# The opening phase of a two-layer transformer kernel: evictions shared by two engines, products with the identity ahead of the turns, one-column sums and a first weight chunk in halves

## The reference, cut to what matters

```python
c_act = jax.nn.silu(c)
mod = c_act @ w_ada + b_ada
shift_mix, scale_mix, gate_mix, ... = jnp.split(mod, N_MOD, axis=-1)
h = rms_norm(x) * (1 + scale_mix) + shift_mix
proj = h @ w_in
# second block, both of its layers (a and b):
kv = rmsnorm(mem, mem_norm) @ w_mem_kv
```

## Time and profile before

| what | value |
|---|---|
| median of 3 runs | 1800.53 us (1800.51 to 1802.06) |
| the profiled execution's own time | 1800.57 us |
| its span, first to last instruction | 1798.9 us |
| TensorE busy | 1768.7 us, 98% of the span |
| VectorE busy | 1096.3 us, 61% |
| ScalarE busy | 733.2 us, 41% |
| share of PE in the chain that ended last | 92% |

### The profile page before, as it was taken

How to read it: one execution, slowest core, us unless ns; L and a number is a source line. 1 busy time by engine, 2 the same in 40 slices (tenths; PEclk the granted TensorE clock), 3 DMA queues, 4 the chain that set the end, 5 groups by cost and what they waited for, 6 DMA issues and landing times.

```text
span 1798.9 us, 22457 instructions
## 1 busy us (share of the span) xinstructions
PE 1768.7 (98%) x8312; PEld 1428.7 (79%) x8312; DVE 1096.3 (61%) x1598; ACT 733.2 (41%) x1030; POOL 40.6 (2%) x78
## 2 busy tenths in 40 slices
PE   7999999999999999999999999999999999999998
PEld 6887547888888888878888888889766888888887
DVE  6878775655556335775677674245577567677423
ACT  7313663333444223444344443233365434444322
POOL 4110000000000000000000000000000000000000
PEclk9999999999999999999999999999999999999999
DMA  9794203232222323312322222323401232222231
GB/s 345 266 340 139 80 21 111 75 106 94 93 93 87 111 82 98 112 48 94 117 93 93 93 93 84 109 83 106 170 24 48 74 114 93 93 93 93 94 105 70
DMA packets 149081, 195.29 MB, mean 109 GB/s; under 512 B 3646, under 2 KB 133000, under 8 KB 146332
## 3 DMA queue, kind: packets, MB, share of 16 engines
q1 hardware_dynamic: 140696, 154.23, 26.4%
q0 software_dynamic: 7600, 39.13, 5.9%
q10 hardware_dynamic: 724, 1.10, 0.2%
HBM read 189.15 MB, written 5.29 MB: 108 GB/s over the span
## 4 chain that ended last, share of the span: by engine, by line
PE 92%; DVE 4%; DMA 2%; ACT 1%; issue 1%; POOL 0%; DVEq 0%; ACTq 0%
PE bank L805 20%; PE bank L807 20%; PE bank L806 20%; PE bank L868 3%; PE bank L870 3%; PE bank L869 3%; PE bank L1475 2%; PE bank L1474 2%; PE bank L1476 2%; PE bank L952 2%; PE bank L1004 1%; PE bank L848 1%; PE bank L973 1%; PE bank L849 1%; PE bank L850 1%; PE bank L1061 1%
## 5 line engine op out<-in xcount | busy, mean ns | idle before, releaser
L1947 DVE TENSOR_TENSOR w_lo<-w_stage,w_hi 128x2048 fp32r<-128x2048 f32 (+3 forms) x136 | 299.0, 2198 | 436.3 <-ACT w_hi L1502 436.0
L805 PE MATMUL bank<-act_hi,w_hi 128*128 128x512 f32 x1216 | 475.2, 391 | 1.5 <-DVE act_lo L2322 0.6
L807 PE MATMUL bank<-act_hi,w_lo 128*128 128x512 f32 x1216 | 473.3, 389 | 0.0
L806 PE MATMUL bank<-act_lo,w_hi 128*128 128x512 f32 x1216 | 473.1, 389 | 0.0
L1502 ACT ACTIVATE w_hi<-w_stage 128x2048 fp32r<-128x2048 f32 (+3 forms) x138 | 253.6, 1837 | 466.0 <-PE bank L807 335.6
L805 PEld LDWEIGHTS bank<-act_hi,w_hi 128*128 128x128 f32 x1216 | 228.2, 188 | 50.7 <-DVE act_lo L2011 2.1
L806 PEld LDWEIGHTS bank<-act_lo,w_hi 128*128 128x128 f32 x1216 | 228.3, 188 | 47.7 <-issue 0.5
L807 PEld LDWEIGHTS bank<-act_hi,w_lo 128*128 128x128 f32 x1216 | 228.2, 188 | 47.7
L805 PE MATMUL bank<-mid_hi,w_hi 128*128 128x512 f32 x352 | 136.9, 389 | 0.0
L806 PE MATMUL bank<-mid_lo,w_hi 128*128 128x512 f32 x352 | 136.9, 389 | 0.0
L807 PE MATMUL bank<-mid_hi,w_lo 128*128 128x512 f32 x352 | 136.9, 389 | 0.0
(11 more groups left out here) (412 smaller groups left out, 2622.8 us busy)
## 6 DMA issues: line engine op xcount, KB each, us to landing
ada_stage<-in_w_ada POOLq DMA_DIRECT2D x24, 1024.0 KB, 7.4
w_stage<-in_w_up SPq DMA_DIRECT2D x22, 1024.0 KB, 5.0
w_stage<-in_a_ffn_in SPq DMA_DIRECT2D x22, 1024.0 KB, 5.0
w_stage<-in_b_ffn_in SPq DMA_DIRECT2D x22, 1024.0 KB, 5.1
w_stage<-in_w_in SPq DMA_DIRECT2D x10, 1024.0 KB, 7.6
w_stage<-in_b_ffn_out SPq DMA_DIRECT2D x10, 1024.0 KB, 5.1
w_stage<-in_w_down SPq DMA_DIRECT2D x8, 1024.0 KB, 5.1
w_stage<-in_a_ffn_out SPq DMA_DIRECT2D x8, 1024.0 KB, 5.1
```

What stands on the lines that cost most here:

```text
L805: pe.matmul(dst, wh, mh, start=start and k == 0, stop=False)
L806: pe.matmul(dst, wh, ml, start=False, stop=False)
L807: last = pe.matmul(dst, wl, mh, start=False, stop=stop and k == nk - 1)
L1947: dve.tensor_tensor(w_lo[slot][:, 0:n], raw[:, 0:n], w_hi[slot][:, 0:n].bitcast(FP32), ALU.subtract).then_inc(w_ready, 1)
```

## The change

It touches only the opening phase.

1. Ahead of the turn of the gains, behind the wait for their rows, TensorE multiplies the identity by itself 16 times (`WARM`), and 8 times more ahead of the turns of `x` (`WARM_X`). Nothing reads the results.
2. The even tiles of the memory are evicted by ACT, the odd ones by DVE.
3. The squares of `x` are summed by ACT (two token tiles) and DVE (two), on both behind their evictions of the memory.
4. ACT computes silu of `c` behind the root of `x`, and one table load is gone.
5. SP issues `w_mem` when the first piece of `w_ada` has landed, instead of at the start.
6. The eight column blocks of `scale_mix` are summed by eight products with a column of ones, one output column each, instead of eight turns and a reduction on DVE.
7. The first chunk is split in halves of 1024 columns, and TensorE goes through it tile k by tile k for both output tiles.

```diff
+WARM, WARM_X = 16, 8
...
+            sp.wait_ge(ada_loaded[0], 16)
+            load_mem(0)
...
             pe.wait_ge(vec_loaded, 16 * (len(VECTORS) + 1))
+            for i in range(WARM):
+                pe.matmul(bank[0][:, 0:P], ident[:, :], ident[:, :], start=True, stop=True)
             sizes = [N_VEC, 48] + [2 * CT] * 6
             batch("vec", 0, [(vec_rows[0:sizes[i], i, :], P * i) for i in range(2)])
...
-                if n >= 2:
-                    pe.wait_ge(tr_saved, n - 1)
+                if k:
+                    pe.wait_ge(*((mem_odd_saved, k // 2) if k in (3, 5, 7) else (tr_saved, n - 1)))
...
+            for i in range(WARM_X):
+                pe.matmul(bank[0][:, 0:P], ident[:, :], ident[:, :], start=True, stop=True)
             pe.wait_ge(x_diag, NT)
...
-            ada_sum(range(8, 16), 2)
+            for j in range(8):
+                last = pe.matmul(bank[2][:, j:j + 1], ada_acc[:, P * (8 + j):P * (9 + j)], one_col,
+                                 start=True, stop=True)
+            last.then_inc(mod_summed, 1)
...
+            pe.wait_ge(w_half, 2)
+            for k in range(KT):
+                if k == KT // 2:
+                    pe.wait_ge(w_ready, 1)
+                for m in range(2):
+                    part(C0["qk_a"], 0, m, [k], act, tile_wait=normed("w_in_scaled") if m == 0 else None,
+                         start=k == 0, stop=k == KT - 1)
...
-            act.preload_act_table(ACT.Silu)
             act.wait_ge(tr_saved, TR0["vec"] + 1)
-            act.activation(sig_c, vec[:, VEC0["c"]:VEC0["c"] + 8], ACT.Silu).then_inc(c_act, 1)
-            act.preload_act_table(ACT.Sqrt)
-            for k in range(KT):
-                if k == 6:
-                    act.wait_ge(x_squared, NT)
-                    act.activation(x_rms, x_ss, ACT.Sqrt, scale=1.0 / D, bias=eps).then_inc(x_root, 1)
+            for k in range(0, KT, 2):
                 act.wait_ge(tr_ready, TR0["mem"] + k + 1)
...
-                last.then_inc(tr_saved, 1)
+                last.then_inc(tr_saved, 2)
+            act.wait_ge(x_loaded, 16)
+            for t in range(2):
+                act.activation(x_junk[t][:, :], x_tok[:, t, :], ACT.Square, accum_out=x_ss[:, t:t + 1])\
+                    .then_inc(x_squared, 1)
+            act.wait_ge(x_squared, NT)
+            act.activation(x_rms, x_ss, ACT.Sqrt, scale=1.0 / D, bias=eps).then_inc(x_root, 1)
+            act.preload_act_table(ACT.Silu)
+            act.activation(sig_c, vec[:, VEC0["c"]:VEC0["c"] + 8], ACT.Silu).then_inc(c_act, 1)
...
+            for k in range(1, KT, 2):
+                dve.wait_ge(tr_ready, TR0["mem"] + k + 1)
+                for l, name in enumerate(("a_mem_norm_2", "b_mem_norm_2")):
+                    last = dve.tensor_scalar(mem_scaled[:, l, k, :], bank[6 + (TR0["mem"] + k) % 2][:, 0:NMEM],
+                                             gain(name, k), None, ALU.mult)
+                last.then_inc(mem_odd_saved, 1)
             dve.wait_ge(x_loaded, 16)
-            for t in range(NT):
-                if t:
-                    dve.wait_ge(x_squared, t)
-                dve.tensor_tensor_reduce(out=x_junk, in0=x_tok[:, t, :], in1=x_tok[:, t, :], scale=1.0,
+            for t in range(2, NT):
+                dve.tensor_tensor_reduce(out=x_junk[t][:, :], in0=x_tok[:, t, :], in1=x_tok[:, t, :], scale=1.0,
```

More of the change, by code:

```diff
@@ L128, in program @@
         sq_junk = at("sq_junk", [P, D], o_x)
+        x_junk = [at(f"x_junk{t}", [P, D], o_act + 4 * KB * t) for t in range(NT)]
         diag = at("diag", [P, NT + 2, P], o_x + 4 * KB)
@@ L242, in program @@
         col_1, col_2, col_12 = stats[:, 36:40], stats[:, 40:44], stats[:, 56:60]
-        x_junk = x[:, 6:8, :].rearrange("p a b -> p (a b)")
         sq = tmp[:, 2:4, :]
@@ L340, in program @@
         w_hi_done = sem("w_hi_done")
-        w_ready = sem("w_ready")
+        w_ready, w_half = sem("w_ready"), sem("w_half")
+        mem_odd_saved = sem("mem_odd_saved")
         tile0_done = sem("tile0_done")
@@ L470, in load_mem @@
                     .then_inc(w_mem_loaded[c], 16)
-            load_mem(0)
             def stream(ph, w, pairs):
@@ L650, in _ @@
             pool.wait_ge(tr_saved, TR0["mem"] + KT)
+            pool.wait_ge(mem_odd_saved, KT // 2)
             for l in range(2):
@@ L1146, in _ @@
                     pe.wait_ge(tr_saved, TR0["mem"] + KT)
+                    pe.wait_ge(mem_odd_saved, KT // 2)
                 if k >= 4:
@@ L1163, in shift_sum @@
                 ada_sum(range(8), 0)
-            for j in range(4):
+            pe.wait_ge(w_half, 2)
[5 more added lines that the diff above has]
+                         start=k == 0, stop=k == KT - 1)
+            for j in range(1, 4):
                 chunk(C0["qk_a"] + j, j % 2, KT, CHUNK_COLS, act, g=G0["qk_a"] + j, gslot=j % 2,
-                      tile_wait=normed(("w_in_scaled", "", "w_in", "")[j]) if j % 2 == 0 else None,
+                      tile_wait=normed("w_in") if j == 2 else None,
                       chunk_wait=(scaled, SPLIT0["w_in_scaled"] + 8) if j == 1 else None,
@@ L1724, in _, with first_half @@
                                           ACT.Copy, scale=gain(name, k))
-                last.then_inc(tr_saved, 1)
+                last.then_inc(tr_saved, 2)
[7 more added lines that the diff above has]
+            act.activation(sig_c, vec[:, VEC0["c"]:VEC0["c"] + 8], ACT.Silu).then_inc(c_act, 1)
+            def first_half(half):
+                part = slice(1024 * half, 1024 * half + 1024)
+                act.activation(w_hi[0][:, part], w_stage[0][:, part], ACT.Copy)\
+                    .then_inc(w_hi_done if half else w_half, 1)
             for k in range(KT):
@@ L1733, in save_x @@
                     act.activation(x[:, k, :], bank[4 + k % 4][:, :], ACT.Copy).then_inc(x_saved, 1)
-            split_at(0)
+            act.wait_ge(w_loaded[0], 16)
+            first_half(0)
             act.wait_ge(scaled, SPLIT0["w_in_scaled"] + 8)
             for t in range(KT):
+                if t == 2:
+                    first_half(1)
                 act.activation(act_hi[:, t, :], x_norm[:, t, :], ACT.Copy, scale=modv(SCALE_MIX, t))\
@@ L2113, in mod_columns @@
                     .then_inc(mod_added, 1)
-                dve.wait_ge(mod_added, n + 1)
+                dve.wait_ge(mod_added, n)
                 dve.tensor_scalar(mod[:, 8 * scale:8 * scale + 8], mod[:, 8 * scale:8 * scale + 8],
@@ L2305, in _, with first_split @@
             dve.wait_ge(mod_summed, 1)
-            dve.tensor_reduce(out=mod[:, 8:16], in_=banks[:, 2:4, :].rearrange("p b (c n) -> p (b c) n", n=P),
-                              axis=AXIS.X, op=ALU.add).then_inc(mod_added, 1)
-            dve.wait_ge(mod_added, 1)
-            dve.scalar_tensor_tensor(out=mod[:, 8:16], in0=mod[:, 8:16], scalar=1.0, in1=vec[:, P + 8:P + 16],
+            dve.scalar_tensor_tensor(out=mod[:, 8:16], in0=bank[2][:, 0:8], scalar=1.0, in1=vec[:, P + 8:P + 16],
                                      op0=ALU.add, op1=ALU.add).then_inc(scaled, 8)
-            split_w(0, 0)
+            def first_split(half):
+                dve.wait_ge(*((w_hi_done, 1) if half else (w_half, 1)))
+                part = slice(1024 * half, 1024 * half + 1024)
+                dve.tensor_tensor(w_lo[0][:, part], w_stage[0][:, part], w_hi[0][:, part].bitcast(FP32),
+                                  ALU.subtract).then_inc(w_ready if half else w_half, 1)
+            first_split(0)
             dve.wait_ge(scaled, SPLIT0["w_in_scaled"] + 8)
@@ L2330, in shift_columns @@
                                   axis=AXIS.X, op=ALU.add).then_inc(mod_added, 1)
-                dve.wait_ge(mod_added, 2)
+                dve.wait_ge(mod_added, 1)
                 dve.tensor_tensor(mod[:, 0:8], mod[:, 0:8], vec[:, P:P + 8], ALU.add).then_inc(mod_ready, 1)
             for t in range(KT):
+                if t == 3:
+                    first_split(1)
                 low_scaled(t)
```

## The result

The changed kernel took **1808.22 us** (median of 6 runs, 1807.73 to 1809.28) against 1800.68 of the kernel before (6 runs on the same chip): ratio 1.0040 [1.0029, 1.0051], 7.5 us slower. The prediction was 1807.0, its range 1803.5 to 1809.6. The profiled execution has a span of 1806.8 us (before: 1798.9), so there are 7.9 us to be found.

A forecast was written before the change was run, and what follows sets the result against it. TensorE, busy 98% of the span, was taken as the bound, so time follows the start of chunk 0: 1800.57 + 7.4 (later start) - 0.85 (waits regained) = 1807.1, predicted as 1807.0 us, range 1803.5 to 1809.6.

The forecast's parts named there:

- rival (b): Opening: clock stays slow or falls in the root's wait; block 6.9 us, even tiles 2.05 each, 1809.6 us; chance 0.09.
- The block is on the path: Behind the gains' wait: 16 products, 11 slow and 5 fast, take 5.9 us unhidden; gains turn at v = 14.1.
- From the gains to the root: Evictions, then squares on both engines: root of `x` 10.2 us after the gains' turn (v), 24.3 instead of 17.56.
- The turns of `x` at the fast pace: TensorE ahead of chunk 0: turns start at 25.8 us, +6.8, and with the last eviction take 8.1 as before.
- 0.6 us of idle time ahead of the sums: TensorE ahead of the scale sums: VectorE's sum over `w_ada` ends 0.5 us late, so 0.6 of new idle time.
- The column products at 1.0 us: Scale sum on TensorE: eight one-column products take 1.0 us, between 1.8 and half of that, replacing turns of 0.91.
- Gains that are hidden: VectorE ahead of chunk 0: parts 6 and 7 shorten its chain, but TensorE's own work hides it; worth nothing.
- Loads: Opening: `w_ada` issued 5.6 us later, last lands by 31, needed at 31.7; late root covers `w_mem`; priced at nothing.
- What comes back: Behind chunk 0: the 0.6 us shifted `act_lo` wait goes and about 0.25 of the 0.3 wait; 0.85 returned.
- (a): Opening: vector rows land earlier, at earliest 5.8 us, without `w_mem` competing; 1807.0 - 2.4 = 1804.6 us; chance 0.10.
- (c): Between 160 and 300 us: waits of 4.0 and 3.9 absorb the delay; half leaves 1803, nearly all 1800.5; chance 0.10.
- (d): Behind chunk 0: 8.8 us of waits absorb the 7.4 delay whole, ending at 1799.2 us; chance 0.05.

The follow-up runs named there:

- the block alone: Kernel before plus only the 16 identity products behind the wait for the gains: 1804.37 us against 1801.50, ratio 1.0018.
- the order alone: Parts 2, 3, 4 and 7 against the kernel before; no identity products, `w_mem` at the start, scale sum turned: 1804.93 us against 1801.27.
- the repaired kernel: Changed kernel with the 16 products ahead of the gains' wait, 20 instead of 8 ahead of `x`, scale sum turned: 1802.56 us against 1800.98 before.
- the filled kernel: Changed kernel with 20 identity products instead of 8 ahead of the turns of `x`: 1810.03 us against 1801.50 of the kernel before.
- the early block: Changed kernel with the 16 identity products moved ahead of the wait for the gains: 1803.14 us against 1801.50 of the kernel before.
- interleaved: Changed kernel with 16 products ahead of the gains' wait, none before `x`, squares between memory evictions, scale sum turned: 1802.17 us against 1801.27 before.
- `w_mem` first: Version with squares between memory evictions and 16 more identity products in TensorE's gaps, `w_mem` load back at the start: 1801.18 us against 1800.99 before.

## Why the prediction was right

Side and size were right: 1808.2 for a predicted 1807.0, +7.5 us for +6.5. The mechanism was right in the main: the block and the late order move chunk 0, and the time follows. One step was wrong, the pace of the turns of `x`, and part of the closeness is luck, since the idle time that was predicted behind them took up 0.6 of its 1.6 us. The time alone would not have told the forecast from rival (b), whose 1809.6 lies nearly as close; the traces do. The steps, one by one.

- **The block is on the path.** Right. Predicted start of the gains' turn 14.1, measured 14.41: 6.2 us instead of 5.9. At 0.214 and 0.111 us a record, 6.18 us for 32 records make 25 slow and 7 fast, so about 13 slow products where I took 11. That close a count is partly luck: the same 32 records took from 5.23 to 6.79 us in the ten profiles that have them. That the block is on the path is shown by the block alone (chunk 0 4.1 us later, time +2.9) and by the block moved ahead of the wait (5.9 back). The rule of the Trainium skill that the prediction weighed (TensorE: Matmul & The Clock Gate, Part 1) held against the row: the end of the block and all turns of the memory behind it were fast.
- **From the gains to the root.** Right: v + 10.2 was predicted, 24.30 - 14.41 = 9.9 measured. The reason given, squares behind evictions instead of beside them, fits the order alone: its root is 3.0 us late with no block, and the turns of `x` cost 1.7 more, since the clock fell in its 4.70 us wait (+3.7 in time). In the repaired kernel, with TensorE fast, the root is 1.5 late. Both kernels have parts 2, 3 and 4 together, so the squares were not told from the sharing.
- **The turns of `x` at the fast pace.** The start was right to 0.1 (25.77), the length wrong: 9.04 for 7.41, +1.63. Rival (b) had named the fall of the clock in the wait for the root, but priced it as a dearer block (6.9 us; it took 6.2) and memory turns at 2.05 us a tile (they came every 1.64), and put nothing on the turns of `x` themselves. My step took one stretch of 7.41 us as a property of these turns, while the same turns took 7.41 in some kernels and 9.04 in others.
- **0.6 us of idle time ahead of the sums.** Not there, because the slow turns reached past the end of VectorE's sum (36.37). With fast turns it is there: 0.64 in the filled kernel and in the one without the block. So the net price of the clock was 1.0, not 1.6.
- **The column products at 1.0 us.** Mis-sized: 1.70 from the first to the next product. The bound of 1.8, one load of weights for each record, was the value: 1.84 us for 16 records. Alone they moved chunk 0 by 1.0; the +0.7 in time is within the noise.
- **Gains that are hidden.** Right: a shorter chain on VectorE brought nothing, since TensorE came to chunk 0 later than its operands.
- **Loads.** Right: priced at nothing, and neither VectorE's sum nor chunk 0 waited for one.
- **Start of chunk 0.** 42.5 predicted, 44.11 measured. The difference is the sum of these misses: +1.63 turns, -0.77 idle time and the two memory products ahead of it, +0.70 columns, +0.08 in the memory products behind them, -0.03 in the start: 1.6.
- **What comes back.** 0.85 predicted, 1.1 measured; the shifted `act_lo` wait vanished as said, the one for `qkv` stayed at 0.3, where 0.25 of it should have gone. In its place the 0.3 us wait for `p_high` went, which the prediction did not name, and 0.2 is not located. That the two sums lie close is luck.
- **The rivals.** (a) falls: the gains' rows landed at 8.23 with `w_mem` issued later, 8.21 with it in the queue behind them. By the rule of ring order (the Trainium skill, DMA: Bandwidth & Descriptors, Queues, rings and completion order) this was to be expected; the trace agrees. (c) and (d) fall: the later waits are unchanged at 4.0 and 3.9.

What stays open: which waits let the clock fall. Behind the same 2.92 us it fell in two profiles (the change, and the early block) and not in a third (the change without the block); behind 0.64 us and the column products it fell in one and not in another; and in the kernel before with the early block it fell after a wait of 1.79 us. There is one profile of each kernel. Why the repaired kernel and the early block end at the same +1.6, though chunk 0 starts at 37.13 in one and 38.63 in the other, is not settled either: the intervals, 0.2 to 3.4 us and 0.7 to 4.0, leave room for the 1.5 us. VectorE's second sum starts at nearly the same time in both (44.78 and 44.92), which fits a second bound but was not tested by itself.

## What to carry to other kernels

Products that are to warm TensorE belong ahead of the wait they are to bridge, not behind it: behind the wait for the gains the same 16 products moved the turn of the gains by about 6 us, and chunk 0 by 4.1 in the kernel before and 5.5 in the change; ahead of it they moved chunk 0 by 0.2. Before taking time out of a row of TensorE, look at when the engine that feeds it ends: here the gain of 1.4 us at chunk 0 came back as 1.4 us of waits, since VectorE's second sum started no earlier. And two engines that share one job gain only if the job was what the next stage waited for; here the squares had been free beside the evictions.

## What the hardware showed that I had not expected

- A product with one output column costs as much as one with 128: eight of them are 16 records and took 1.84 us, 0.11 a record, nearly the same as in the turns of `x` (64 records in 7.41 us). The eight turns that they replaced are one record each and took 1.06.
- The granted clock of the views says nothing about the first microseconds. In the block it read 1.00 while records lasted 421 ns (median) against 275 in the memory's turns behind it. The trace's first record of the clock lies at 13.55 us in the changed kernel, inside the block, and at 18.68 in the one before, between the last slow turn of the memory and the fast turns of `x`; ahead of it the views print 1.00 without a record. The prediction's reading of the earlier trace rows, 1.00 for the first 19 us, was no reading of the clock. In later stretches (0.67, 0.50) it fell with the pace.
- A stretch that was filled does not keep the clock for the next one: with the wait ahead of the turns of `x` filled, the low level came one stage later (granted 0.82 and 0.75 from 36 to 44 us), behind 0.64 us of waiting and the one-column products. With turned sums behind the same wait it did not come, but neither did it with the one-column sums in the kernel without the block. One profile each, so this is an observation and not a rule.
- The clock can fall far from the edit too. In four profiles (without the block, filled wait, interleaved, `w_mem` first) it fell between 272 and 285 us, and the products on `sb_pl` took 55.1 or 55.2 us from first to last; in the other ten they took 53.4 or 53.5. That 1.7 us is as large as several of the effects measured here.
